# Input projection of the even layer: chunks five to sixteen in three rounded products, context caches fetched later

## The reference

```python
qa, ka, va, z, af, ab, bf, bb, qb, kb, vb = split_cols(h @ w_in, EVEN_IN_SIZES)
qkv = short_conv(jnp.concatenate([qa, ka, va], axis=-1), conv_w)
```

## Time and profile before

| | us |
|---|---|
| median of 3 runs | 2656.54 |
| lowest, highest | 2654.82, 2658.88 |
| profiled execution, its own time | 2652.94 |
| its span | 2651.1 |
| TensorE busy | 2358.5 (89%) |
| VectorE, ScalarE, GpSimd busy | 1009.2, 867.9, 456.8 |

### The profile page before, as it was taken

One profiled execution on the slowest core, in us unless ns is written; L12 is line 12 of the kernel. 1 busy time (PEld: TensorE's weight loads), 2 busy tenths in 40 slices (PEclk: granted clock), 3 DMA queues, 4 the chain that ended last, 5 costly groups with the idle time before them and its releaser, 6 DMA issues.

```text
span 2651.1 us, 34319 instructions
## 1 busy us (share of the span) xinstructions
PE 2358.5 (89%) x13870; PEld 1983.6 (75%) x13871; DVE 1009.2 (38%) x1457; ACT 867.9 (33%) x1237; POOL 456.8 (17%) x258
## 2 busy tenths in 40 slices
PE   6999987748899999989889999869898888898994
PEld 3777665538767999989866566669797778897883
DVE  2211265455723122142101343133345676634544
ACT  2211234212114111131222232133345666644544
POOL 0000001463002000020000000033214444423311
PEclk8998987759999999999999999969999999999997
DMA  7111102950421122112211000026447788866755
GB/s 286 49 63 49 40 32 90 346 192 24 165 98 64 64 80 80 53 51 77 86 44 50 17 1 1 0 118 228 172 171 259 294 320 315 321 207 222 254 184 167
DMA packets 70074, 353.62 MB, mean 133 GB/s; under 512 B 12112, under 2 KB 17872, under 8 KB 37296
## 3 DMA queue, kind: packets, MB, share of 16 engines
q1 hardware_dynamic: 65200, 337.28, 34.8%
q0 software_dynamic: 4736, 14.26, 1.5%
HBM read 318.06 MB, written 33.46 MB: 133 GB/s over the span
## 4 chain that ended last, share of the span: by engine, by line
PE 62%; issue 16%; POOL 9%; DVE 6%; ACT 4%; DMA 2%; SPq 0%; POOLq 0%; DVEq 0%; ACTq 0%
PE ps L558 59%; POOL wring_x L1845 5%; PE ps L695 1%; PE ps L913 1%; POOL tmp L1069 1%; ACT arena L965 1%; POOL tmp L1067 1%; POOL arena_x L1556 1%; DMA xT<-in_x 1%; DVE tmp L1354 1%; DVE att L935 1%; DVE tmp L1294 1%; DMA wring<-in_w_mod 1%; POOL rows L2028 0%; ACT hT L686 0%
## 5 line engine op out<-in xcount | busy, mean ns | idle before, releaser
L558 PE MATMUL ps<-hT,wring 128*128 128x320 f32 x1472 | 405.7, 438 | 12.3 <-ACT hT L686 10.6
L558 PEld LDWEIGHTS ps<-hT,wring 128*128 128x128 f32 x1472 | 283.4, 193 | 134.7 <-issue 20.2
L1845 POOL TENSOR_TENSOR wring_x<-wring,arena_x 128x2048 fp32r<-128x2048 f32 (+1 forms) x60 | 276.4, 4615 | 495.8 <-ACT arena_x L1839 495.8
L558 PE MATMUL ps<-arena_x,hT_x 128*128 128x256 f32 x2464 | 328.9, 291 | 20.9 <-issue 20.9
L558 PEld LDWEIGHTS ps<-arena_x,hT_x 128*128 128x128 f32 x2464 | 311.2, 196 | 24.5 <-issue 22.4
L1839 ACT ACTIVATE arena_x<-wring 128x2048 fp32r<-128x2048 f32 x153 | 283.3, 1854 | 93.0 <-DMA wring<-in_w_mgu 92.2
L558 PE MATMUL ps<-arena_x 128*128 128x512 f32 (+2 forms) x1144 | 255.8, 378 | 29.1 <-DVE arena_x L2014 13.3
L558 PEld LDWEIGHTS ps<-arena_x 128*128 128x128 f32 x1144 | 205.3, 203 | 60.4 <-issue 25.3
L1845 DVE TENSOR_TENSOR wring_x<-wring,arena_x 128x2048 fp32r<-128x2048 f32 (+1 forms) x90 | 222.8, 2476 | 69.4 <-ACT arena_x L1839 69.4
L558 PE MATMUL ps<-arena 128*128 128x128 f32 (+3 forms) x680 | 174.3, 413 | 7.1 <-ACT arena L965 4.8
L558 PE MATMUL ps<-wring_x,hT_x 128*128 128x256 f32 x1120 | 151.9, 284 | 2.9 <-POOL wring_x L1845 2.9
(11 more groups left out here) (290 smaller groups left out, 2903.7 us busy)
## 6 DMA issues: line engine op xcount, KB each, us to landing
wring<-in_w_mgu SPq DMA_DIRECT2D x105, 1024.0 KB, 5.7
wring<-in_w_mod SPq DMA_DIRECT2D x48, 1024.0 KB, 9.7
wring<-in_w_mdn SPq DMA_DIRECT2D x30, 1024.0 KB, 5.2
wring<-in_w_gu SPq DMA_DIRECT2D x22, 1024.0 KB, 4.8
wring<-in_w_mdn SPq DMA_DIRECT2D x20, 768.0 KB, 4.3
wring<-in_w_ev SPq DMA_DIRECT2D x14, 1024.0 KB, 5.2
rows<-hT SPq DMA_DIRECT2D x1, 12288.0 KB, 34.9
wring<-in_w_dn SPq DMA_DIRECT2D x16, 704.0 KB, 4.2
```

Of the source, the lines that this page charges most:

```text
L558: return nc.tensor.matmul(out, lhsT, rhs, start=first, stop=last)
L1845: eng.tensor_tensor(wslot_x[s][:, 0:size], wslot[s][:, 0:size], whi[b % 6][:, 0:size].bitcast(F32), ALU.subtract).then_inc(ready, 1)
```

## The change

For blocks two to seven (chunks five to twelve of q, k, v and the four of z) each float32 product becomes three products of rounded operands, as in the feed-forward. ScalarE rounds h into `h_hi` (eight copies) and each weight block into `ehi` (three buffers, used in turn; from block five on it waits until TensorE has finished the chunk that read the buffer before). GpSimd makes `h_lo` by eight subtractions. VectorE subtracts `ehi` from the block in place. The new buffers lie in areas that the later stages use: `h_hi` in `tmp`, `h_lo` and `ehi` in the arena where `kT` and `vB` lie, so the fetch of the caches moves behind the last z chunk.

```diff
--- before.py
+++ after.py
@@ -256,6 +256,8 @@
         dhi = exact((FC + 2) * T, 4, LK * P)
         sg = arena[:, FC * T:(FC + 2) * T].rearrange("p (b t) -> p b t", b=2)
         fhi = exact((FC + 2) * T, 3, WB)
+        h_hi, h_lo = fh[0], exact(10240, KD, T)
+        ehi = [exact(15872, 3, WB)[:, s, :] for s in range(3)]
 
         qn, qr, kn, vC = chunks(0, HC, T), chunks(5120, 4, T), chunks(7680, HC, TK), chunks(13824, NT + 1, 1024)
         krT, ckv, cq = arena[:, 19968:19968 + TK], chunks(20736, 2, TK), chunks(22272, 3, T)
@@ -302,6 +304,8 @@
             sem(n) for n in ("ya_ready", "yc_ready", "fsq_ready", "out_ready"))
         dhi_ready, dlo_ready, lead_ready, left_ready, left_pool_ready = (
             sem(n) for n in ("dhi_ready", "dlo_ready", "lead_ready", "left_ready", "left_pool_ready"))
+        ex_hi_ready, ex_lo_ready, ehi_ready, elo_ready = (
+            sem(n) for n in ("ex_hi_ready", "ex_lo_ready", "ehi_ready", "elo_ready"))
         hlo_ready, fhi_ready, flo_ready = sem("hlo_ready"), sem("fhi_ready"), sem("flo_ready")
 
         ahi_ready = sem("ahi_ready")
@@ -763,14 +767,21 @@
 
         def pe_even_in():
             pe_first("qkv", 4, 0)
-            for c in range(4, 12):
-                if c % 2 == 0:
-                    w = block("qkv", c // 2)
-                pe_linear("qkv", c, 0, cols(w, KD, 256, c % 2), from_h)
-            for c in range(4):
-                if c % 2 == 0:
-                    w = block("z", c // 2)
-                pe_linear("z", c, 0, cols(w, KD, 256, c % 2), from_h)
+            for n in range(2, EX):
+                for u in range(2):
+                    stage, c = ex_chunk(n, u)
+                    s = take(stage, c)
+                    for prod, (w, h, ready) in enumerate(((ehi[n % 3], h_hi, ehi_ready), (ehi[n % 3], h_lo, ehi_ready),
+                                                          (wring_x[:, ex_slot(n), :], h_hi, elo_ready))):
+                        if u == 0:
+                            nc.tensor.wait_ge(ready, n - 1)
+                        for k in range(KD):
+                            if n == 2 and u == 0 and prod < 2:
+                                nc.tensor.wait_ge(ex_lo_ready if prod else ex_hi_ready, k + 1)
+                            for half in range(2):
+                                last = mm(pair(s)[:, half, :], w[:, k * 256 + u * P:k * 256 + (u + 1) * P],
+                                          h[:, k, half * HT:(half + 1) * HT], prod + k == 0, prod == 2 and k == KD - 1)
+                    filled(last, stage, c)
             w, s = block("gat", 0), take("gat", 0)
             for t in range(NT):
                 for k in range(KD):
@@ -796,8 +807,45 @@
                                   w[b][:, k * 256:(k + 1) * 256], k == 0, k == KD - 1)
                 last.then_inc(ps_full[s], 1)
 
+        EX = 8
+
+        def ex_chunk(n, u):
+
+            return ("qkv", 2 * n + u) if n < 6 else ("z", 2 * (n - 6) + u)
+
+        def ex_slot(n):
+            return wuse("qkv", n)[0] if n < 6 else wuse("z", n - 6)[0]
+
+        def act_ehi(act, n):
+
+            s, use = wuse("qkv", n) if n < 6 else wuse("z", n - 6)
+            act.wait_ge(w_full[s], 16 * (use + 1))
+            if n >= 5:
+                full(act, *ex_chunk(n - 3, 1))
+            nc.scalar.activation(ehi[n % 3], wring[:, s, :], ACT.Copy).then_inc(ehi_ready, 1)
+
+        def dve_elo(dve, n):
+
+            dve.wait_ge(ehi_ready, n - 1)
+            s = ex_slot(n)
+            nc.vector.tensor_tensor(wring_x[:, s, :], wring[:, s, :], ehi[n % 3].bitcast(F32), ALU.subtract
+                                    ).then_inc(elo_ready, 1)
+
+        def pool_ex_lo(pool):
+            for k in range(KD):
+                pool.wait_ge(ex_hi_ready, k + 1)
+                nc.gpsimd.tensor_tensor(h_lo[:, k, :], hT[:, k, :], h_hi[:, k, :].bitcast(F32), ALU.subtract
+                                        ).then_inc(ex_lo_ready, 1)
+
         def act_even_in(act):
+            for k in range(KD):
+                act.wait_ge(h_ready, k + 1)
+                nc.scalar.activation(h_hi[:, k, :], hT[:, k, :], ACT.Copy).then_inc(ex_hi_ready, 1)
+            act_ehi(act, 2)
+            act_ehi(act, 3)
             for c in range(12):
+                if c % 2 == 0 and 4 <= c // 2 + 3 < EX:
+                    act_ehi(act, c // 2 + 3)
                 s = full(act, "qkv", c)
                 nc.scalar.activation(raw[:, 1:1 + SEQ], ps[:, s, 0:SEQ], ACT.Copy)
                 nc.scalar.activation(raw[:, 2 + SEQ:2 + HT], ps[:, s, SEQ:HT], ACT.Copy)
@@ -838,7 +886,11 @@
             nc.vector.tensor_tensor(dst[:, SEQ:T], dst[:, SEQ:T], rtmp, ALU.add).then_inc(ps_free[s], 1)
 
         def dve_even_in(dve, st):
+            dve_elo(dve, 2)
+            dve_elo(dve, 3)
             for c in range(12):
+                if c % 2 == 0 and 4 <= c // 2 + 3 < EX:
+                    dve_elo(dve, c // 2 + 3)
                 done(dve, "qkv", c)
                 if c:
                     dve.wait_ge(qkv_ready, c)
@@ -2187,6 +2239,8 @@
 
         @block_.gpsimd
         def _(pool):
+            pool_ex_lo(pool)
+            full(pool, "z", 3)
             pool.dma_start(kT[:, :, T:TK], I["ck"]).then_inc(caches_in, 16)
             pool.dma_start(vB[:, NT, :], I["cv"]).then_inc(caches_in, 16)
 
```

## The result

The changed kernel takes 2625.59 us (median of 4 runs, 2614.96 to 2635.47) against 2655.68 for the kernel before beside it: a ratio of 0.9878, interval 0.9845 to 0.9911. A second measurement gave 2624.55 and 0.9901 (0.9876 to 0.9925). The profiled run took 2624.85 us.

What follows compares the result with a forecast made beforehand. The prediction took TensorE's time per chunk to bound the projection stage; 18.9 us there plus 1.3 us in the head made 20.2 us, turning the median 2656.54 into 2636.3 us, range 2630 to 2644.

Steps and rivals of the forecast that it cites:

- Twelve chunks, 18.9 us: First projection, chunks five to sixteen: three rounded products (7.04 us) replace one full-precision product (8.61 us), saving 18.9 us.
- the closer matmuls of the last rival: Projection stage: a rounded chunk takes 6.46 us, the stage gives 25.8 us, total 2629.4 us; chance 0.01.
- The lower price: Rounded matmuls in the projection: 135.8 ns each instead of 147, three products 6.52 us, saving an estimated 25.1 us.
- Head, 1.3 us: Start of the kernel: two 256 KB cache transfers leave the full DMA ahead of tokens x, saving 1.3 us.
- The rival with the empty head: Start of the kernel: moving the caches gives nothing, only the projection counts, 2637.6 us; chance 0.13.
- New work at no cost: Projection: added ScalarE roundings (done near 70 us), GpSimd subtractions (near 80) and VectorE subtractions delay nothing.
- VectorE's 2.31 us per subtraction: Projection: each of VectorE's six subtractions of weight blocks was priced at 2.31 us.
- The drain: Rival, projection: ScalarE and VectorE pairs cost over 14.1 us, TensorE waits for PSUM slots, about 2649 us; chance 0.03.
- the clock over the rounded chunks: Rival, projection: TensorE's clock falls to 0.50, chunks cost up to 14.1 us, about 2721 us; chance 0.03.
- The lower clock that was allowed for behind the stage: Gate projection, granted clock 0.66 before: places where the clock falls and rises may shift; 2 us in the range.
- Attention near 321: Sign of the forecast: attention begins near 321 us, where it began at 341.01 before.
- All later waits are between engines or for weights that a finished chunk releases, so they move with it: After the projection: later work moves earlier with the chunks, so the whole 20.2 us reaches the end.

Runs made afterwards that it cites:

- a127: The changed kernel with 127 more TensorE instructions (satisfied waits) ahead of the expert loop; 2636.75 us, ratio 0.9926 to the kernel before.
- b86h: The kernel before with 86 more TensorE instructions (satisfied waits) in two idle places of its head; 2634.35 us, ratio 0.9914.
- b256: Control: the kernel before with 256 more TensorE instructions (satisfied waits), one whole 16 KB block, in idle stretches; 2660.2 us, ratio 1.0015.
- a213: The changed kernel with 213 more TensorE instructions, placed three ways: 63 before the feed-forward (no time given), all before the gather (2622.58 us), 140 in the head (2614.66 us).
- a84: The changed kernel with 84 more TensorE instructions (satisfied waits) before the expert loop's first gather; slow branches 29.5 us, no kernel time given.

## Why the prediction was wrong

- *Twelve chunks, 18.9 us:* right, 18.91 by the start of the gates. The price of 2.347 us per product from the feed-forward carried over exactly; the closer matmuls of the last rival (6.46 us a chunk) did not come. The lower price that the prediction took from the Trainium skill, page "TensorE: Matmul & The Clock Gate", section "Back-to-back issue gap", is given there for a matmul by itself; for a stream of weight loads and matmuls the section says that both set the spacing. It was no price for this stage, which the prediction did not say.
- *Head, 1.3 us:* right, 1.12 with the change and 1.01 alone. The rival with the empty head falls.
- *New work at no cost:* right. ScalarE ended 2 us and GpSimd 4 us before the times named. VectorE's 2.31 us per subtraction was low (3.57) while GpSimd subtracts, inside the cover that was named.
- *The drain, the clock over the rounded chunks:* neither came. TensorE has no gap between 53.25 and 189.08. The lower clock that was allowed for behind the stage came in the gates: that projection took 14.41 us, before 12.94.
- *Attention near 321:* 320.91.
- *"All later waits are between engines or for weights that a finished chunk releases, so they move with it":* **this is the step that failed.** It counted what later work waits for in data. TensorE also waits for its own instructions when it branches, and that wait depends on how many instructions stand in front of the loop, which the change altered by 385. Slow branches fell from 27.7 to 13.6 us, TensorE's idle time by 9.8 and its busy time, for the same matmuls at a higher clock, by 5.8; the loop became 22.1 us shorter in the profiled pair (809.2 to 787.1). Some 7 of these were worth nothing: they are the last pair of slow branches (3780 and 3172 ns), which stand behind the last item, where the end of the kernel waits for transfers and VectorE.
- The lead along the profiled run, by the same work of VectorE in both traces: 20.1 us at the attention, 14.8 at the loop's first items, 30.4 behind the loop (2618.7 before, 2588.3 after), 28.1 at the end of the span. The loss of 5 in the middle does not come in every execution: most of it is there by 627.7 before, which is 613.8 after, while the same kernel profiled again reaches that point at 609.2. The loop then gave 15.6.

The forecast 2636.3 was the right answer for this change at the old place: a127, changed but with its loop at 127, measured 2636.75. That they agree to half a microsecond is partly luck, since a127 pays 3 us for its waits. The rows that would have told of the loop were in the trace of before: three waits of 5.3 to 5.7 us on "issue" behind long items, and branches of 3 to 4 us beside others of 79 ns. I had not asked which of a later stage's waits depend on the length of the code.

What is shown is that the branches' time goes with the place of the loop's code, that a move of 256 or 512 brings the same branches back, and that a slow branch overlaps the arrival of an instruction packet. Which branches find their code already there, and why, is argued only. The Trainium skill, page "Advanced Engine Details and Errata", section "ISA Cache", has 128 KB on TensorE in lines of 16 KB with 256 instructions; page "Runtime: NRT & Kernel Launch", section "Instruction fetch mechanics", says that a taken branch whose target is not in the current window of two pages stalls until that page is fetched. The packets of 16 KB with 259 instructions and the packets in the slow branches agree. The window of two does not: the second long item of the changed kernel, about 1450 records from 1877.4 to 1976.2 us, ran without one instruction packet. The second page gives 2048 instructions for TensorE; the trace counts about 1475 records in a turn with the long body and 793 in one with the short, so by an estimate from these the two together would exceed it by some 200. No run made the loop smaller, so that this is the reason stays open.

## What to carry to other kernels

An edit that adds or removes instructions ahead of a loop with conditional bodies shifts the loop's code; in this kernel that alone was worth 21 us (86 instructions, b86h); before such a gain or loss is credited to the edit, compare the branches of the loop in both traces, price them by the idle time behind them and not by their records, and measure both versions with the code at the same place. If a trace shows branches of microseconds on the engine that sets the time, a few satisfied waits put where that engine is idle may be worth as much as the edit itself; they must be placed anew after every later edit. TensorE's price per product, taken from another stage of the same trace with the same shapes and the same clock, held to a per cent; the prices of GpSimd (2.36 us, measured 2.02) and VectorE (2.31, measured 3.57 while GpSimd worked) did not.

## What the runs showed of the hardware

- A TensorE branch of this loop took some 80 to 480 ns, or 1.6 to 6.6 us with an instruction packet under way, by the place of the loop's code. The same branches were slow at three distances 256 apart (place 127: before, b256, a127) and at two 512 apart (place 213: b86h and the three a213 kernels).
- A slow branch of 3.2 to 4.4 us by itself cost TensorE 1.1 to 2.0 us of idle time, a pair 5.3 to 5.9.
- Satisfied waits are not free on a busy path: two of them make one instruction, and these begin 109 ns apart. 426 before the gather fill 23.1 us and cost about 10, 254 cost 3; during the rest TensorE was waiting anyway.
- The clock can fall in one execution and not in another at the same work. TensorE at 1470 to 1490 us, changed kernel and a213, whose code is the same up to there but for 63 instructions:

```profile
1470.00:1490.00 20.00, 19.83 (x101) 12.12 (x100) 8.38 (x22) 7.58 (x18) 0.00 (x0) 1.00 0.00 1
```

```profile
1470.00:1490.00 20.00, 20.00 (x57) 10.84 (x56) 5.19 (x12) 4.32 (x10) 0.00 (x0) 0.57 0.00 1
```

  It cost a213 some 10 us there, and a84, which has exactly the changed kernel's code up to there, lost as much. So one profiled run is no measure of a difference under 10 us in this kernel; the start of the attention repeats within 2 us over the ten profiled executions that share the code up to it.
